# State space mixer: masked decay and scaled values split into f16 halves, three f16 products a head at step 13 in place of one f32 product at step 11

## What is computed

```
cs = jnp.cumsum(dt * a, axis=2)
xdt = xs * dt[..., None]
decay = jnp.exp(jnp.where(causal, seg, -jnp.inf))
cb = jnp.einsum('bclgn,bcsgn->bcgls', cm, bm)
y_intra = jnp.einsum('bcgjls,bcsgjp->bclgjp', cb[:, :, :, None] * decay, xdt)
states = jnp.einsum('bclgn,bclgj,bclgjp->bcgjpn', bm, decay_end, xdt)
...
y = y_intra + y_inter + d_skip * xs
```

## Time and profile before

| | |
|---|---|
| median of 3 runs | 1997.5 us (1995.81 to 1997.83) |
| profiled execution, own time | 1992.77 us |
| its span | 1991.1 us |
| mean granted TensorE clock | 0.996 |
| PE busy | 1937.7 us (97%) |
| DVE busy | 1189.5 us (60%) |
| ACT busy | 969.8 us (49%) |
| POOL busy | 473.0 us (24%) |
| 8 slots of layer 1, and the two norm panels | 209.05 to 350 us of the span |
| the same of layer 2 | from 1197.91 us |

### The profile page before, as it was taken

How to read it: one execution, slowest core, us unless ns; L and a number is a source line. 1 busy time by engine, 2 the same in 40 slices (tenths; PEclk the granted TensorE clock), 3 DMA queues, 4 the chain that set the end, 5 groups by cost and what they waited for, 6 DMA issues and landing times.

```text
span 1991.1 us, 27991 instructions
## 1 busy us (share of the span) xinstructions
PE 1937.7 (97%) x11102; PEld 1057.7 (53%) x11102; DVE 1189.5 (60%) x1477; ACT 969.8 (49%) x1793; POOL 473.0 (24%) x298
## 2 busy tenths in 40 slices
PE   6999999999999999999979999999999999999998
PEld 3446665455456665544444466654554566655443
DVE  6676766377436766544366768663773366765434
ACT  5774333356325666543347643433653356665323
POOL 0213443133212222111002134522331222221110
PEclk9999999999999999999989999999999999999999
DMA  5224222343334443234132242123433343432441
GB/s 185 85 85 128 64 85 64 117 117 88 104 101 124 120 117 112 85 127 143 54 108 80 69 131 82 64 85 101 117 101 104 104 131 98 115 107 85 154 139 42
DMA packets 205519, 205.14 MB, mean 103 GB/s; under 512 B 29504, under 2 KB 196423, under 8 KB 205383
## 3 DMA queue, kind: packets, MB, share of 16 engines
q1 hardware_dynamic: 205383, 203.29, 33.3%
HBM read 176.00 MB, written 4.19 MB: 91 GB/s over the span
## 4 chain that ended last, share of the span: by engine, by line
PE 42%; DVE 5%; ACT 2%; issue 1%; DVEq 0%; ACTq 0%
PE PS L477 40%; DVE wsp L1028 1%; DVE X L1031 1%; ACT X L888 1%; DVE M L1028 1%; DVE Y L1028 0%; PE PS L665 0%; DVE small L1031 0%; DVE small L1121 0%; PE PS L743 0%; ACT wsp L770 0%; PE PS L711 0%; ACT X L773 0%; PE PS L583 0%; DVE Y L1031 0%
## 5 line engine op out<-in xcount | busy, mean ns | idle before, releaser
L477 PE MATMUL PS<-hT,wsp 128*128 128x512 f16 x4896 | 1082.3, 379 | 0.0
L477 PEld LDWEIGHTS PS<-hT,wsp 128*128 128x128 f16 x4896 | 475.9, 98 | 561.4 <-issue 11.2
L1028 DVE SCALAR_TENSOR_TENSOR wsp<-stage,wsp 128x2048 f16<-128x2048 f32 x150 | 384.9, 2566 | 199.5 <-ACT wsp L770 198.3
L477 PE MATMUL PS<-ys,wsp 128*128 128x512 f16 x1536 | 340.0, 379 | 0.0
L770 ACT ACTIVATE wsp<-stage 128x2048 f16<-128x2048 f32 x150 | 285.3, 1902 | 90.7 <-PE PS L477 86.8
L477 PEld LDWEIGHTS PS<-ys,wsp 128*128 128x128 f16 x1536 | 149.6, 98 | 177.8 <-issue 3.0
L477 PE MATMUL PS<-wsp,hT 128*128 128x256 f16 x1728 | 194.5, 273 | 0.0
L477 PEld LDWEIGHTS PS<-wsp,hT 128*128 128x128 f16 x1728 | 168.7, 98 | 23.6 <-issue 2.3
L1345 POOL TENSOR_TENSOR M<-M,T 128x512 f32<-128x512 f32 x48 | 69.6, 1456 | 342.8 <-DVE T L1028 342.8
L1345 POOL TENSOR_TENSOR X<-X,K 128x1024 f32<-128x1024 f32 x26 | 62.9, 2421 | 349.2 <-DMA X<-X 349.2
L773 ACT ACTIVATE X<-PS 128x512 f32<-128x512 f32 x120 | 68.6, 593 | 123.7 <-PE PS L477 90.9
(11 more groups left out here) (186 smaller groups left out, 2036.5 us busy)
## 6 DMA issues: line engine op xcount, KB each, us to landing
stage<-w_in SPq DMA_DIRECT2D x122, 1024.0 KB, 5.1
stage<-w_branch SPq DMA_DIRECT2D x32, 1024.0 KB, 5.0
X<-X SPq DMA_DIRECT2D x120, 128.0 KB, 2.3
stage<-w_out SPq DMA_DIRECT2D x8, 1024.0 KB, 5.7
out<-xres SPq DMA_DIRECT2D x8, 512.0 KB, 2.6
Y<-Y SPq DMA_DIRECT2D x24, 128.0 KB, 2.3
xres<-x SPq DMA_DIRECT2D x4, 512.0 KB, 4.9
Y<-T SPq DMA_DIRECT2D x16, 128.0 KB, 2.5
```

Source lines behind the costliest of these rows:

```text
L477: return pe.matmul(o, a, b, start=start, stop=stop, skip_group_check=True)
L1028: return dve.scalar_tensor_tensor(out=o, in0=a, scalar=c, in1=b, op0=op0, op1=op1)
```

## The change

The f32 product of `between(p)` is made of f16 halves. Both operands are split: ScalarE copies `xdt` and then `est` to f16 (the high halves), GpSimd subtracts for the low half of `xdt` (after `xw`, ahead of the triangles), VectorE subtracts for the low half of `est` (after `split_lo`). TensorE waits for `ssd_ml` and `ssd_xl`, the low halves, and issues three f16 matmuls for each of 8 heads, 24 of 128x64, where there were 8 in f32. `between` moves from step 11 to step 13 in the slots; `middle` stays at 14. The halves lie in parts of tiles T and M that are free in these slots.

```diff
     if p in SSD_SLOT:
-        return 11, 14
+        return 13, 14
...
+        xdt16 = T[:, 512:1024].bitcast(F16).rearrange("p (h n) -> p h n", h=2)
+        decay16 = M[:, 6:8, :].rearrange("p a b -> p (a b)").bitcast(F16).rearrange("p (h j l) -> p h j l", h=2, j=8)
...
-                    pe.wait_ge(s["ssd_mt"], q + 1)
-                    pe.wait_ge(s["ssd_x"], q + 1)
+                    pe.wait_ge(s["ssd_ml"], q + 1)
+                    pe.wait_ge(s["ssd_xl"], q + 1)
                     for j in range(8):
-                        mm(PS[:, 4, HD * j:HD * j + HD], est[:, j, :], xdt[:, j, :], True, True)
+                        o, chans = PS[:, 4, HD * j:HD * j + HD], slice(HD * j, HD * j + HD)
+                        mm(o, decay16[:, 0, j, :], xdt16[:, 0, chans], True, False)
+                        mm(o, decay16[:, 0, j, :], xdt16[:, 1, chans], False, False)
+                        mm(o, decay16[:, 1, j, :], xdt16[:, 0, chans], False, True)
...
                 for n in splits_in(p):
                     split_hi(n)
+                if p in SSD_SLOT:
+                    q = SSD_SLOT.index(p)
+                    act.wait_ge(s["ssd_x"], q + 1)
+                    copy(xdt16[:, 0], xdt.rearrange("p j n -> p (j n)")).then_inc(s["ssd_xh"], 1)
+                    act.wait_ge(s["ssd_mt"], q + 1)
+                    copy(decay16[:, 0].rearrange("p j l -> p (j l)"), est.rearrange("p j l -> p (j l)")).then_inc(s["ssd_mh"], 1)
                 before(p)
...
                     for n in splits_in(p):
                         split_lo(n)
+                if p in SSD_SLOT:
+                    q = SSD_SLOT.index(p)
+                    dve.wait_ge(s["ssd_mh"], q + 1)
+                    tt(decay16[:, 1], est, decay16[:, 0], ALU.subtract).then_inc(s["ssd_ml"], 1)
                 scans(p)
                 before(p)
...
                     tt(xw, xdt, head(dend[:, c, hs]), ALU.mult).then_inc(s["ssd_x"], 1)
+                    pool.wait_ge(s["ssd_xh"], q + 1)
+                    tt(xdt16[:, 1], xdt.rearrange("p j n -> p (j n)"), xdt16[:, 0], ALU.subtract).then_inc(s["ssd_xl"], 1)
                     if q < 7:
                         triangle(q + 1)
```

More of the change, by code:

```diff
@@ L309, in program @@
                  "rope_dma", "rope_sin", "rope_done", "rope_hi", "rope_lo", "rope_stack",
-                 "ssd_tri", "ssd_x", "ssd_g", "ssd_exp", "ssd_mt", "ssd_y", "ssd_read", "ssd_out", "ssd_st", "ssd_ss", "ssd_norm", "ssd_T",
+                 "ssd_tri", "ssd_x", "ssd_g", "ssd_exp", "ssd_mt", "ssd_mh", "ssd_ml", "ssd_xh", "ssd_xl", "ssd_y", "ssd_read", "ssd_out", "ssd_st", "ssd_ss", "ssd_norm", "ssd_T",
                  "yb_hi", "yb_lo", "sw_vE", "sw_s", "sw_m", "sw_e", "sw_n", "sw_T", "sw_Ta", "sw_o", "sw_y",
```

## The result

| | before | the change |
|---|---|---|
| median of 4 runs each | 1997.65 us (1995.81 to 1997.83) | 2009.16 us (2009.04 to 2009.43) |
| ratio, 95% interval | | 1.0068 [1.0056, 1.008] |
| profiled execution, its span | 1992.77, 1991.1 | 2009.05, 2007.2 |
| mean granted clock of TensorE | 0.996 | 0.992 |

The change is slower by 11.5 us by the medians, whose quotient is 1.0058; that lies inside the interval of the ratio. The forecast was 8 us slower, 2005.5, and the range, 1993 to 2014, holds the time. The two spans lie 16.1 us apart: the profiled execution of before was 4.9 under its median, that of the change 0.1 under.

A forecast was written before the change was run, and what follows sets the result against it. TensorE, busy 97% of the span, was taken as the bound, with thin cover where VectorE and GpSimd are full. Terms -8.2 + 4.5 + 3.4 + 2.8 + 0.8 + 0.7 = +4.0 a layer, +8.0 in all: 2005.5 us, range 1993 to 2014.

The forecast's parts named there:

- the turn: VectorE and GpSimd: an instruction of one with two SBUF operands waits until the other's is over; they alternate.
- It waits 5.2 us where it waited 0.67: +4.5: Slot 17: TensorE reaches its transposes at 234.7, VectorE's state stands at 239.9; +4.5 us a layer.
- f16 product, 8 slots: TensorE: 24 f16 matmuls in 0.71 us replace the f32 product's 1.73, 1.02 us a slot; -8.2 us a layer.
- slot 18, wait: Slot 18's transposes: VectorE's state stands 16.1 us in, TensorE is there at 12.7; +3.4 us a layer.
- starts of slots 23 and 24: First matmuls wait for VectorE's PSUM read, covered by three steps instead of five, plus the turn; +2.8 us a layer.
- low halves late in 23 and 24: Step 13 of slots 23 and 24: low halves stand 9.9 us in, TensorE arrives at 9.5; +0.8 us a layer.
- norm panel: Panels 20 and 25: the norm's chain hangs on a last ssd_y some 0.3 us later; +0.7 us for both.
- The busy sum: Sign of a right forecast: TensorE's busy sum 16 us lower.
- Rival 1: Slots 17 and 18: the two M<-M products pass the second triangle, 1.83 us less wait each; 1998.2 us, chance 0.14.
- Rival 2: Slots 17 and 18: the halves don't need the turn, transposes wait 1.1 us each; 1989.5 us, chance 0.11.
- Rival 3: Low halves on GpSimd and VectorE take 0.3 to 0.5 us more than their nearest forms; 2010 us, chance 0.15.
- Rival 4: TensorE: short matmuls with their own weight loads go slowly, from the f32 product's 1.73 us up; 2017 us, chance 0.02.

The follow-up runs named there:

- E4: The change, with GpSimd's two triangles in slots 17 and 18 held until VectorE has made both M<-M products: 1996.08 us, ratio 1.0.
- E1: The kernel before with only the f32 product moved from step 11 to step 13, no halves: 2006.66 us, ratio 1.006.
- E3: The change plus 17 f16 matmuls of 512 columns that nobody reads, ahead of slot 17's transposes: 2002.32 us, ratio 1.0036.
- E8: Control: the kernel before, with only the triangles of slots 17 and 18 held until both M<-M products are made: 1993.57 us, ratio 0.999.
- E5: The change with the f16 product back at step 11 instead of 13: 2008.97 us, ratio 1.0071.
- E2: The change with its halves made and waited for, but the f32 product in place of the 24 f16 matmuls: 2019.33 us, ratio 1.0119.
- E6: The change only in slots 16, 19, 21 and 24; the other four keep the f32 product at step 11: 1992.03 us, ratio 0.9983.
- E7: E6 with the triangles of slots 17 and 18 held until both M<-M products are made: 1990.79 us, ratio 0.998.

## Why the prediction was right, and where it was off

**Sign and mechanism: right.** TensorE's gain is real and VectorE's chain takes more than it back. E4 shows the turn at work: the same instructions, in an order in which they don't meet in slots 17 and 18, cost +0.8 instead of +11.5. The turn needs the move beside it: E1 costs +11.4 with the turn as it was, by the cover that the two steps gave.

**That the time came so near is in part luck.** The rows of the forecast are those of one profiled execution, 1992.77 us, and it said 2000.8 for that. The change's profiled execution took 2009.05, which is 16.3 more instead of 8.0. The 8 us were then added to a median (1997.5) that lay 4.7 above the profiled execution; the change's own median lies 0.1 above its profiled one. So the difference of the medians, 11.5, is smaller than what the slots show, 13.6 from the first slot's start to the transposes of panel 25 in both layers, and nearer to the 8.0 forecast.

**The step that failed: "It waits 5.2 us where it waited 0.67: +4.5", taken as the whole price of slot 17's wait.** The sum has no term for what TensorE's granted clock does behind such a wait. The waits themselves were 1.31 and 3.74 us, 5.05 together, and with the gaps around them +4.5, as forecast. But the transposes and the six matmuls behind them ran at 0.52 instead of 1.00, 0.83 and 1.27 us more, so slot 17 grew by 5.65 instead of 3.5. In layer 2 the low clock cost 3.87 - 2.19 = 1.7 us at the same place (1236.94 to 1240.81). E3 shows that it was this: with TensorE kept busy the clock stays, slot 17 lasts 20.22 us (3.54 more than before's, 3.5 forecast), and the time is +7.0. Before's own trace had a sign of it: behind the 12.03 us of idle between the layers, the matmuls from 1006 to 1011 ran at 0.52.

Term by term for layer 1, forecast and measured (differences of slot lengths; the clock's part is the change's slot 17 less E3's):

| Term | forecast | measured |
|---|---|---|
| f16 product, 8 slots | -8.2 | -8.0 |
| slot 17, waits | +4.5 | +4.5 |
| slot 17, lower clock | none | +2.1 |
| slot 18, wait | +3.4 | +3.3 |
| starts of slots 23 and 24 | +2.8 | +2.6 |
| low halves late in 23 and 24 | +0.8 | +1.4 |
| norm panel | +0.7 (both) | +0.7 (panel 20) |
| layer | +4.0 | +6.9 |

The measured terms add to 6.6; 0.3 is spread over the slots. Panel 25 waits 0.17 us more and lies behind the stretch that the 6.9 covers. Layer 2 has the same terms, but 1.7 instead of 2.1 for the lower clock.

- **VectorE's chain in slot 17** was worked out almost to the row: `est` times `gm` over at 227.0 forecast, 227.05 measured (227.93 less the 0.88 us by which this execution's slots start later), the state's reading over at 239.9 forecast, 240.0 measured.
- **Slot 18** has a smaller wait than forecast, 2.28 instead of some 3.4, yet the right length, 2.32 us longer where 3.4 less 1.0 was forecast. Its matmuls ahead of step 0 took 1.95 us at the lower clock instead of 1.08, TensorE came 0.9 us later, and the wait took that in (the 3.3 of the table is 2.45 of gap and this 0.87). The state stands 16.06 us into the slot; 16.1 was forecast.
- **Low halves late.** Forecast 0.4 in each of two slots, measured 1.1 in slot 23 (0.96 idle ahead of the 24 matmuls) and 0.3 in slot 24. This term was too small by 0.6 a layer.
- **The busy sum** was to fall by 16 us and fell by 6.9. Matmuls at the lower clock are counted as busy: the two stretches in slot 17 and the one at 1435 put some 6 us back. The remaining 3 I can't place. That sum was a poor test.
- **The stretch at 1435** cost some 1.5 us more. It stands behind a wait that before has as well:

The change, then before, PE's timeline in the local attention of layer 2:

```profile
1434.18 1.25 PE L585 MATMUL PS<-K,X 128*128 128x128 f32 x8 [1.93 <-DVE X L1039]
```

```profile
1419.76 1.06 PE L583 MATMUL PS<-K,X 128*128 128x128 f32 x8 [1.92 <-DVE X L1028]
```

In one the clock falls behind it, in the other it doesn't. At the same place it fell in E8 (behind 1.94 us) and not in E3, E4 and E5 (1.93 to 1.96). I have no run that tells what decides.

**The rivals.** Rival 1 (the `M<-M` products pass the second triangle) is half seen: in slot 17 one of the two was held and one ran free once the triangles were over (the forecast had given "only one `M<-M` held" as a sign of this rival), in slot 18 both were held, 4.68 us. Nothing passed the triangle: the chain still ended where forecast. Rival 2 (the halves don't need the turn) fell: `M<-Y,M` took 2.91 us with a triangle beside it and 1.21 without. Rival 3 (longer low halves) had the right time, 2010, for another reason: alone they take 1.21 and 1.23, against 1.22 and 1.17 reckoned. Rival 4 (slow short matmuls) fell with 0.70 us for 24, 29 ns each.

The Trainium skill, "TensorE: Matmul & The Clock Gate", in the section on the back-to-back issue gap, has about 81 ns for a weight load and a matmul of 128 columns in a sustained stream. An estimate by it for these 24 matmuls of 64 columns was 1.94 us. The measurement decides: 0.70.

**Against the expectation, E1.** The change's +11.5 and E1's +11.4 are the same, and so one could think that only the move matters. E2 shows the three parts: the move costs 11.4, the halves on top of it 12.7, and the f16 product takes 10.2 back. Those add to 13.9 and not 11.5, since the change was measured apart, beside a before that was 2.4 us slower than the one beside E1 and E2.

## What to carry to other kernels

Where TensorE is 97% busy in a fixed order, a shorter product only pays in the steps whose VectorE and GpSimd chain has slack. Work out for each step when the chain ends, with every added instruction's effect on the turn between VectorE and GpSimd (here the order of two triangles was worth 11 us), and use the new form only where TensorE arrives later: E6 and E7 beat both kernels, the change everywhere lost. Where a change opens a wait on TensorE, allow for a slower clock behind it: here it fell behind 3.74 us in both layers, and behind shorter waits at times. It came to between 1.4 and 2.1 us each time that the clock fell on work that could not wait, and to nothing where TensorE would have waited anyway (E2's slot 17).

## What the runs showed of the hardware

- **A long wait costs beyond itself.** Behind 3.74 us of idle, granted clock 0.52 for 6.8 us in layer 1, and 0.50 for about 3.4 us in layer 2, with the same instructions ahead of it. I did not expect two lengths for one cause.
- **Filler work pays.** 17 matmuls that nobody reads (about 3.7 us; with three of the panel's, 20 in 4.48) made the kernel faster by 4.5 us, each set against its own before, or 6.8 between the medians.
- **Behind shorter waits the clock may fall or not.** In the profiled executions it fell behind 2.52 and 2.60 us in both layers of E5, and behind 2.36 and 2.44 in E7. Behind E4's 2.85 and E2's 1.30 and 0.95 (slots 17 and 23) it fell in layer 1 and not in layer 2, behind E1's 1.96 in layer 2 and not in layer 1, and behind E2's 2.64 not at all. At one place of the local attention it fell behind 1.93 us in the change and 1.94 in E8, and did not behind 1.92 in before. What decides is left open. Each of these falls lasted about 3.4 us.
- **The scatter of one kernel goes with its clock.** Of before's 26 runs beside E5 to E8, three had a mean granted clock of 0.996 and took 1992.09 to 1993.12 us, fifteen had 0.994 and took 1994.15 to 1996.39, seven had 0.993 and took 1996.09 to 1997.98. Before's profiled execution had 0.996. That its median is 4.9 higher fits falls of the clock that this execution did not have; only profiled executions show where they are, so that is not shown.
- **The turn holds whatever the type**: f32 products, subtractions into f16, f16 triangles; only operations that read PSUM passed freely. GpSimd is held just as VectorE is: the two triangles take 3.75 us in E4 and 6.78 in the change, where VectorE offers one instruction after another.
